# A streaming transformer kernel: the first stream unit's steps in another order on four engines

## Chip, cores, metric

One core of one Trainium2 chip. The metric is the device time of one execution of the whole program, in microseconds. It computes in fp32, with most products written as three matmuls of split operands (high by high, low by high, high by low).

## What is computed

Two layers of an encoder trunk. Each layer projects the hidden rows, attends in two head groups (latent attention over all cached keys, sliding-window attention with sinks), normalises and mixes the two results, adds the residual, and runs a SwiGLU feed-forward block. The part that the change touches is the attention of the eight running streams ("sample") and the output projection after it:

```
def _sample_layer(x, ckv_c, kr_c, k_c, v_c, p):
    q_lat, q_rope, ckv, kr, sq, sk, sv = _project(x, pos, w_in, q_g, w_uq, w_uk, kv_g)
    o_lat = _mla_attend(q_lat, q_rope, jnp.concatenate([ckv_c, ckv], axis=1),
                        jnp.concatenate([kr_c, kr], axis=1), None)
    o_swa = _swa_attend(sq, jnp.concatenate([k_c, sk], axis=1),
                        jnp.concatenate([v_c, sv], axis=1), sinks, None)
    y = _block_out(x, o_lat, o_swa, p)
...
def _block_out(x, o_lat, o_swa, p):
    o_a = jnp.einsum('bthl,lhv->bthv', o_lat, w_uv).reshape(b, t, MLA_OUT)
    mix = jnp.concatenate([rms_norm(o_a, g_a), rms_norm(o_swa, g_b)], axis=-1)
    x = layer_norm(ALPHA * x + jnp.einsum('btm,md->btd', mix, w_out), ln1_g, ln1_b)
...
```

## The kernel before

Each layer runs in stages: A projects ten row tiles, B attends for the eight prompt tiles, C (the stage of the change) attends for the streams, and then comes the feed-forward block. Stage C has nine units, n = 0 to 8. Unit 0 is the sixteen meta rows, which are short; units 1 to 8 are the eight streams, each with 1040 cached keys. Beside the attention of unit n, stage C multiplies row tile n-1 by `w_out` (1024 by 1024), so that TensorE (PE) has something to do during a softmax. The row tiles 0 to 7 are the prompt's, whose attention is done.

Every engine has its own program, written out by hand, and an engine executes in order: an instruction that waits holds up all that stands behind it. Nothing plans the order; it is the order of the calls at lines 2007 to 2047 (ScalarE, ACT), 2709 to 2752 (VectorE, DVE), 3471 to 3488 (PE) and 1328 to 1368 (SyncE, SP, which issues the loads). Engines wait for each other through counting semaphores. The steps, by the names of the helpers:

- `q_latent_hi/lo`, `q_turned` (ACT L1914, L1920, DVE L2566): the streams' queries are copied out of PSUM, as a high and a low part. `scores(0)` waits for all of them.
- `stream_keys`, `keys_hi`, `keys_lo`: keys of a unit are loaded (`dkraw`, `dsraw`), then split on ACT (`dkh`) and GpSimd (POOL, `dkl`). `four_rotary`, `rotary_hi`, `rotary_lo`, `stream_rotary`: the rotary keys of four units are loaded (`krraw`), split into `krh` on ACT and `krl` on DVE, and three DMAs of SP (L1269) copy the rows of one unit into `drs`. `scores(n)` for n of 1 and more waits for `drs` (semaphore `dr_in0` or `dr_in1`) and for `dkl`.
- `scores(n)` on PE (L3300); `bias(n)` on DVE (L2574, the row maxima; its last instruction writes `nbs`); `soft(n)` on ACT (L1926, the exponentials); `inverse(n)` on DVE (L2588, normalises `Pb`); `turn_probs(n)` on PE (L3342, transposes `Pb`); `turned_hi(n)` on ACT and `turned_lo(n)` on DVE (the split copy `PT`); `values(n)` on PE (L3351); `out_hi(n)` and `out_lo(n)`.
- `mix_load(s)`, `mix_sq(s)` (ACT), `mix_eps(s)` and `mix_norm(s)` (DVE, with a root on POOL between them), `mix_T(s)` on PE (L3393, eight transposes of `mt`), `mix_hi(s)` on ACT (`mTh`), `mix_lo(s)` on DVE (`mTl`): row tile s is normalised, turned and split for the output projection.
- `w_out_load(k)` on SP, `w_out_hi(n)` on ACT (L1954, writes `wouth`), `w_out_lo(n)` on DVE (L2699, writes `woutl`): the eight 128-row blocks of the matrix are loaded (`woraw`) and split. ACT waits for groups of blocks: the first three in the order of use have one semaphore. `w_out(s, k0, k1)` on PE (L3404) multiplies row tile s by blocks k0 to k1-1: six matmuls of 512 columns for a block. It waits for `mTl` and, in tile 0, for each block's `woutl`.
- `values_hi(b)` on ACT and `values_lo(b)` on POOL split the values of a stream (`dv`).

In units 1 to 8 PE executes `scores(n)`, `w_out(n-1, 0, 5)`, `turn_probs(n)`, `w_out(n-1, 5, 8)`, `values(n)`, `mix_T(n)`.

Of the kernel before, what the change touches and what calls it, by code (L numbers as in the profile page):

```python
# [96 lines left out]
def rows(t):  # L97
    return META if t == TILES - 1 else P
# [27 lines left out]
W_OUT_ORDER = (2, 3, 4, 5, 6, 0, 1, 7)  # L126
# [175 lines left out]
def program(nc, X, LNP, ROT, W_IN, QKVG, W_UQ, W_UK, W_UV, SINKS, MIXG, W_OUT, LN1, W_FF,  # L302
# [8 lines left out]
    with ExitStack() as ctx:  # L311
        names = {}

        def S(name):
            if name not in names:
                names[name] = ctx.enter_context(nc.semaphore(name))
            return names[name]
# [309 lines left out]
        def f(ap):  # L627
            return ap.bitcast(F32)
# [287 lines left out]
        def load_params(sp, l, which):  # L916
            for dst, src in small_loads(l, which):
                sp.dma_start(dst, src, allow_slow_non_contiguous=which == "C").then_inc(S("params_in"), 16)
# [4 lines left out]
        def params(eng, key):  # L923
            eng.wait_ge(S("params_in"), 16 * param_count[key])
# [213 lines left out]
        def _(sp):  # L1138
            for l in range(L):
# [71 lines left out]
                def mix_pair_store(x):  # L1211
                    p, s = PASSES[x][1] // 2, PASSES[x][1] % 2
                    sp.wait_ge(S("b_item_lo"), by_dve(l, ITEM["ot", x]))
                    dst = MIX[BANK * s:BANK * (s + 1), P * p:P * (p + 1)].rearrange("(t p) c -> p t c", p=P)
                    sp.dma_start(dst, mixP[:, :, :]).then_inc(S("b_mixP_out"), 16)
# [30 lines left out]
                def stream_keys(b):  # L1246
                    i = b % 2
                    sem = S(f"dm_in{i}")
                    if b >= 2:
                        sp.wait_ge(S("s_done"), U(l, b - 1) + 1)  # L1250
                    sp.dma_start(dkraw[i][:, :], CKVT[l, b]).then_inc(sem, 16)
                    for j in range(2):
                        sp.dma_start((dsraw[i] if b else dsraw0)[HD * j:HD * (j + 1), :, :],
                                     SKT[l, b].rearrange("(g d) n -> d g n", d=HD)).then_inc(sem, 16)
# [37 lines left out]
                def w_out_load(k):  # L1292
                    sp.dma_start(woraw[:, k, :], w_out_rows[:, k, :]).then_inc(S(f"wo_in{W_OUT_GROUP[k]}"), 16)

                def mix_load(s):
                    t, r = row_tile(s), rows(row_tile(s))
                    if 1 <= s < 9:
                        sp.wait_ge(S("c_ms"), A(l, s))
                        sp.wait_ge(S("c_mT"), A(l, s))
                    if s < 8:  # L1300
                        sp.dma_start(mt[:, :], MIX[cols(t), :]).then_inc(S("mt_in"), 16)
                        return

                    for i in range(2):
                        units = range(i, 1 if s == 8 else UNITS, 2)
                        sp.wait_ge(S(f"mixs_out{i}"), 16 * ([5, 4][i] * l + len(units)))
                    sp.dma_start((mt[0:r, 512:1024] if s == 8 else mtw[:, :]), MIX[cols(t), 512:1024])\
                      .then_inc(S("mt_in"), 16)
# [17 lines left out]
                            sp.wait_ge(S("s_done"), U(l, NB) + 1)  # L1326
                        sp.dma_start((xin, xin_late)[g][i][0:rows(t), :], H1[cols(t), :]).then_inc(S("xin_in"), 16)
                four_rotary(0)
                stream_keys(0)
                for i in range(2):  # L1330
                    sp.dma_start(f(sqT[i][:, :]), SQT[8 + i, :, 0:SWA_H * rows(8 + i)]).then_inc(S("sq_in"), 16)
                mix_load(0)
                load_params(sp, l, "E")
                for k in W_OUT_ORDER[0:2]:
                    w_out_load(k)
                sp.wait_ge(S("qa"), 2 * (l + 1))
                sp.wait_ge(S("qr"), 2 * (l + 1))
                sp.wait_ge(S("qa_rope"), 2 * (l + 1))
                sp.dma_start(mixg[:, :], MIXG[l:l + 1, :].to_broadcast([P, D])).then_inc(S("mixg_in"), 16)
                mix_pair_store(NPASS - 1)  # L1340
                stream_rotary(0)
                for k in W_OUT_ORDER[2:5]:
# [339 lines left out]
        def _(act):  # L1682
            for l in range(L):
# [200 lines left out]
                def keys_hi(b):  # L1884
                    i = b % 2
                    act.wait_ge(S(f"dm_in{i}"), 16 * 3 * (l * NB // 2 + b // 2 + 1))
                    act.activation(dkh[i][:, :], dkraw[i][:, :], ACT.Copy).then_inc(S("dm_hi"), 1)
                    act.activation(dsh[i][:, :, 0, :], (dsraw[i] if b else dsraw0)[:, :, :], ACT.Copy).then_inc(S("dw_hi"), 1)

                def rotary_hi(x):  # L1890
                    act.wait_ge(S("kr_in"), 16 * (2 * l + x + 1))
                    if x == 0:
                        act.wait_ge(S("qa"), 2 * (l + 1))
                        act.wait_ge(S("qr"), 2 * (l + 1))
                    act.activation(krh[:, :], krraw[:, :], ACT.Copy).then_inc(S("kr_hi"), 1)
# [46 lines left out]
                def turned_hi(n):  # L1942
                    if n >= 1:
                        act.wait_ge(S("pv"), U(l, n - 1) + 1)
                    for g in groups_of(n):
                        act.wait_ge(S("probsT"), G(l, n, g) + 1)
                        src, dst = turned(n, g, PT[:, 0, :])
                        act.activation(dst, src, ACT.Copy).then_inc(S("probsT_hi"), 1)
# [5 lines left out]
                def w_out_hi(n):  # L1954
                    k = W_OUT_ORDER[n]
                    act.wait_ge(S(f"wo_in{W_OUT_GROUP[k]}"), 16 * W_OUT_GROUP.count(W_OUT_GROUP[k]) * (l + 1))
                    act.activation(wouth[:, k, :], woraw[:, k, :], ACT.Copy).then_inc(S("wo_hi"), 1)

                def mix_sq(s):
                    r = rows(row_tile(s))  # L1960
                    act.wait_ge(S("mt_in"), 16 * (A(l, s) + 1))
                    parts = [mt[0:r, 0:512], mt[0:r, 512:1024]]
                    if s >= 8:
                        act.wait_ge(S("oa"), 2 * l + s - 7)
                        parts[0] = o_of(NB)[0:r, :]
                    if s == 9:
                        parts[1] = mtw[:, :]
                    junk = junkC[:, :].bitcast(mybir.dt.bfloat16)
                    for i in range(2):
                        ins = act.activation(junk[0:r, 512 * i:512 * i + 512], parts[i], ACT.Square,  # L1970
                                             scale=512 ** -0.5, accum_out=ms[s % 2][0:r, i:i + 1])
                    ins.then_inc(S("c_ms"), 1)

                def mix_hi(s):
                    r = rows(row_tile(s))
                    act.wait_ge(S("c_mT"), A(l, s) + 1)
                    if 1 <= s < 9:
                        act.wait_ge(S("c_y"), A(l, s))
                    act.activation(w_out_half(s)[0][:, :, 0:r], heads(OO, r), ACT.Copy).then_inc(S("c_mh"), 1)
# [32 lines left out]
                q_rope_hi(1)  # L2012
                act.wait_ge(S("phase_done"), 5 * phase_no(l, "B"))
                q_nope_hi(1)
                rotary_hi(0)
                q_latent_hi(0)
                keys_hi(0)
                q_turned(0)
                q_turned(1)
                q_latent_hi(1)  # L2020
                mix_sq(0)
                params(act, (l, "E"))
                soft(0)
                for k in range(2):
                    w_out_hi(k)
                turned_hi(0)
                mix_hi(0)
                out_hi(0)
                for k in range(2, 6):
                    w_out_hi(k)  # L2030
                for n in range(1, UNITS):
                    if n >= 2:
# [182 lines left out]
        def _(dve):  # L2215
# [13 lines left out]
            for l in range(L):  # L2229
# [484 lines left out]
                q_rope_lo(1)  # L2714
                dve.wait_ge(S("phase_done"), 5 * phase_no(l, "B"))
                q_nope_lo(1)
                rotary_lo(0)
                q_latent_lo(0)
                q_latent_lo(1)
                params(dve, (l, "E"))  # L2720
                dve.tensor_scalar(nsink[:, :], sinkT[:, 4:5], -1.0, None, ALU.mult).then_inc(S("nsinks"), 1)
                mix_eps(0)
                bias(0)
                mix_norm(0)
                inverse(0)
                w_out_lo(0)
                turned_lo(0)
                mix_lo(0)
                out_lo(0)
                for k in range(1, 5):  # L2730
                    w_out_lo(k)
                for n in range(1, UNITS):
                    if n >= 2:
# [232 lines left out]
        def _(pe):  # L2966
# [8 lines left out]
            for l in range(L):  # L2975
# [497 lines left out]
                q_latent(1)  # L3473
                for n in range(UNITS):
                    scores(n)
                    if n >= 1:
                        w_out(n - 1, 0, K_SOFT)
                    if n == NB:
                        project(1)
                    if n == 0:  # L3480
                        mix_T(0)
                    turn_probs(n)
                    if n >= 1:
                        w_out(n - 1, K_SOFT, KD)
                    values(n)
                    if n >= 1:
                        mix_T(n)
# [208 lines left out]
```

## Time and profile before

| | |
|---|---|
| median of 3 executions | 3064.08 us (3055.17 to 3064.78) |
| the profiled execution, its own time | 3059.69 us |
| its span | 3057.9 us |
| PE busy | 2896.3 us, 95% |
| DVE / ACT / POOL busy | 71% / 41% / 57% |
| TensorE's granted clock, mean | 0.973 |

Busy times are of one profiled execution; a busy PE is not PE at its peak. The granted clock is a share of 2.4 GHz: 1.00 is the full level and 0.50 the level of 1.2 GHz. Times in the rows below are in us from the start of the span. "Idle before" in brackets says how long the engine had stood and what ended that, with the releaser inferred from semaphores.

### The profile page before, as it was taken

The page shows a single profiled execution, that of the slowest core. Times are in us where ns is not written, and L with a number is a line of the kernel's source. Part 1 is how long each engine was busy: PE and PEld are TensorE (multiplying, and loading weights), DVE is VectorE, ACT ScalarE, POOL GpSimd, SP SyncE. Part 2 cuts the span into 40 slices and gives each one's busy share as a digit, 9 for nine tenths or more (in the row PEclk, how much of TensorE's full clock was granted, in tenths as well). Part 3 has the DMA queues.
Part 4 walks back from the last instruction along what each step waited for, and adds up shares of the span by engine and source line. Part 5 has one row for each costly group of instructions (what it writes and reads, how often), then busy time and mean ns, then how long its engine had stood idle before and what let it go on. Part 6 is the DMA issues. An engine that isn't in the chain of part 4 may idle for free.

```text
span 3057.9 us, 54602 instructions
## 1 busy us (share of the span) xinstructions
PE 2896.3 (95%) x20464; PEld 2639.4 (86%) x20464; DVE 2156.6 (71%) x3903; ACT 1256.0 (41%) x2474; POOL 1728.1 (57%) x1388
## 2 busy tenths in 40 slices
PE   7989997999999999999989899989999999999997
PEld 6966665887999999999989666668889999999997
DVE  6767777667777767778655677776577777678777
ACT  3334344445444434444333344444454444344442
POOL 2323333436777767888632233433277777678875
PEclk9989998999999999999989899989999999999998
DMA  4321114553333343333322211156432333433331
GB/s 168 135 86 51 44 40 158 162 161 111 108 105 106 109 164 134 107 104 109 127 93 97 87 42 42 36 173 180 148 116 96 109 110 107 182 111 114 101 104 57
DMA packets 193137, 336.06 MB, mean 110 GB/s; under 512 B 57200, under 2 KB 112752, under 8 KB 190800
## 3 DMA queue, kind: packets, MB, share of 16 engines
q1 hardware_dynamic: 166528, 276.94, 28.2%
q10 hardware_dynamic: 17248, 30.28, 2.7%
q0 software_dynamic: 9136, 25.89, 2.2%
q8 instruction: 135, 2.21, 0.3%
q14 instruction: 90, 0.74, 0.1%
HBM read 263.48 MB, written 65.52 MB: 108 GB/s over the span
## 4 chain that ended last, share of the span: by engine, by line
PE 79%; DVE 10%; issue 3%; ACT 2%; DMA 2%; POOL 2%; SPq 1%; POOLq 0%; DVEq 0%; ACTq 0%
PE PS L2969 23%; PE PS L2971 22%; PE PS L2970 22%; PE PS L3096 5%; DVE mxc L2466 2%; DVE Ph L2505 1%; POOL Pl L1555 1%; PE PS L3364 1%; DMA winraw<-in_W_IN 1%; DMA ht<-in_X 1%; PE PS L3257 1%; DMA woraw<-in_W_OUT 1%; PE PS L2989 0%; DVE T L2778 0%; PE PS L3347 0%
## 5 line engine op out<-in xcount | busy, mean ns | idle before, releaser
L1608 POOL TENSOR_TENSOR wopl<-T,woph 128x512 fp32r<-128x512 f32 x348 | 525.0, 1527 | 98.0 <-ACT woph L2066 97.0
L1555 POOL TENSOR_TENSOR Pl<-Pf,Ph 128x256 fp32r<-128x256 f32 (+5 forms) x174 | 218.9, 1265 | 366.4 <-DVE Ph L2505 366.4
L2969 PE MATMUL PS<-hidh,wdh 128*128 128x320 f32 (+1 forms) x1408 | 419.3, 298 | 5.4 <-DVE hidl L2783 4.4
L2971 PE MATMUL PS<-hidh,wdl 128*128 128x320 f32 (+1 forms) x1408 | 418.9, 298 | 0.0
L2970 PE MATMUL PS<-hidl,wdh 128*128 128x320 f32 (+1 forms) x1408 | 418.2, 297 | 0.0
L2066 ACT ACTIVATE woph<-T 128x512 fp32r<-128x512 f32 x348 | 216.6, 630 | 475.9 <-DVE T L2778 259.6
L2969 PE MATMUL PS<-xoh,woph 128*128 128x320 f32 x1232 | 383.1, 311 | 3.5 <-POOL wopl L1608 3.1
L2971 PE MATMUL PS<-xoh,wopl 128*128 128x320 f32 x1232 | 381.2, 309 | 0.0
L2970 PE MATMUL PS<-xol,woph 128*128 128x320 f32 x1232 | 380.5, 309 | 0.0
L2836 DVE TENSOR_TENSOR acc<-acc,PS 128x320 f32<-128x320 f32 (+1 forms) x608 | 275.4, 455 | 148.4 <-PE PS L2971 145.5
L2969 PE MATMUL PS<-x_both,woph 128*128 128x264 f32 x1232 | 349.9, 284 | 0.0
L2971 PE MATMUL PS<-x_both,wopl 128*128 128x264 f32 x1232 | 349.7, 284 | 0.0
L2970 PE MATMUL PS<-x_both,woph 128*128 128x264 f32 x1232 | 349.2, 283 | 0.0
L1615 POOL TENSOR_TENSOR wdl<-rd,wdh 128x512 fp32r<-128x512 f32 x176 | 256.7, 1478 | 30.3 <-ACT wdh L2075 30.3
L2969 PEld LDWEIGHTS PS<-hidh,wdh 128*128 128x128 f32 x1408 | 266.0, 189 | 7.7 <-issue 4.7
L2971 PEld LDWEIGHTS PS<-hidh,wdl 128*128 128x128 f32 x1408 | 265.9, 189 | 0.0
L2970 PEld LDWEIGHTS PS<-hidl,wdh 128*128 128x128 f32 x1408 | 265.8, 189 | 0.0
L1608 POOL TENSOR_TENSOR wopl<-rg,woph 128x512 fp32r<-128x512 f32 x128 | 178.9, 1399 | 130.3 <-ACT woph L2066 130.3
L1873 ACT ACTIVATE Pf<-PS 128x512 f32<-128x512 f32 (+5 forms) x174 | 127.8, 752 | 277.9 <-PE PS L3096 277.3
L2969 PEld LDWEIGHTS PS<-xoh,woph 128*128 128x128 f32 x1232 | 232.3, 189 | 6.0 <-POOL wopl L1608 4.9
L1608 POOL TENSOR_TENSOR wopl<-ru,woph 128x512 fp32r<-128x512 f32 x132 | 189.3, 1442 | 84.7 <-ACT woph L2066 82.3
L2970 PEld LDWEIGHTS PS<-xol,woph 128*128 128x128 f32 x1232 | 232.5, 189 | 0.2
(498 smaller groups left out, 7829.1 us busy)
## 6 DMA issues: line engine op xcount, KB each, us to landing
ru<-in_W_FF SPq DMA_DIRECT2D x88, 512.0 KB, 4.3
rd<-in_W_FF SPq DMA_DIRECT2D x176, 256.0 KB, 2.7
rg<-in_W_FF SPq DMA_DIRECT2D x82, 512.0 KB, 4.2
xs_scratch<-x_part ACTq DMA_DIRECT2D x56, 264.0 KB, 2.5
x_both<-xs_scratch ACTq DMA_DIRECT2D x14, 1056.0 KB, 7.8
sqt_scratch<-sqTs POOLq DMA_DIRECT2D x18, 512.0 KB, 4.6
hc<-out_H SPq DMA_DIRECT2D x18, 512.0 KB, 3.7
dkraw<-in_CKVT SPq DMA_DIRECT2D x16, 520.0 KB, 4.5
```

What stands on the lines that cost most here:

```text
L1555: ins = pool.tensor_tensor(Pl[i][0:kk, 1, c], Pf[i][0:kk, 1, c], f(Ph[i][0:kk, 1, c]), ALU.subtract)
L1608: pool.tensor_tensor(wopl[k][:, :, :], w_whole(w, k, first), f(woph[k][:, :, :]), ALU.subtract)\
L1615: pool.tensor_tensor(wdl[:, n, e, :], rd[n][:, :, :], f(wdh[:, n, e, :]), ALU.subtract)\
L1873: ins = act.activation(Pf[r][0:kk, :, c], both_banks(u)[0:kk, :, c], ACT.Exp)
L2066: act.activation(woph[k][:, :, :], w_whole(w, k, first or second), ACT.Copy).then_inc(S("f_hi"), 1)
L2466: dve.tensor_reduce(mxc[s][:, u["tl"], :, u["c"]], both_banks(u)[:, :, 0:u["c1"] - u["c0"]], AX.X, ALU.max, negate=True).then_inc(S("b_ite ...
L2505: ins = dve.tensor_copy(Ph[r][0:kk, :, c], Pf[r][0:kk, :, c])
L2836: dve.tensor_tensor(a, a, down_bank(u, g), ALU.add).then_inc(S("f_y"), 1)
L2969: pe.matmul(out, wh, mh, start=start, stop=False)
L2970: pe.matmul(out, wh, ml, start=False, stop=False)
L2971: return pe.matmul(out, wl, mh, start=False, stop=stop)
L3096: ins = pe.matmul(out(h), w(rows_, h), x(rows_, h), start=start and n == 0, stop=stop and n == len(passes) - 1)
```

## The change

It reorders calls, in both layers, and adds or removes none. On SP, the streams' window queries `sqT` are loaded ahead of the first keys, the sink parameters ahead of `mt`, and `mixg` ahead of the first two blocks of `w_out`. On ACT, the rotary and key splits go behind the query copies, `mix_sq(0)` behind `soft(0)`, and the first two `w_out_hi` to the other six, behind `mix_hi(0)`; `out_hi(0)` now stands ahead of `mix_hi(0)`. On DVE, `rotary_lo(0)` goes behind the query copies, `bias(0)` and `inverse(0)` ahead of the mix tile's steps, `out_lo(0)` ahead of `mix_lo(0)`, and the first `w_out_lo` to the other four, behind `mix_lo(0)`. On PE, `mix_T(0)` moves from behind `scores(0)` to behind `scores(1)`.

```
@@ SP
                 four_rotary(0)
-                stream_keys(0)
                 for i in range(2):
                     sp.dma_start(f(sqT[i][:, :]), SQT[8 + i, :, 0:SWA_H * rows(8 + i)]).then_inc(S("sq_in"), 16)
+                stream_keys(0)
+                load_params(sp, l, "E")
                 mix_load(0)
-                load_params(sp, l, "E")
-                for k in W_OUT_ORDER[0:2]:
-                    w_out_load(k)
                 ...
                 sp.dma_start(mixg[:, :], MIXG[l:l + 1, :].to_broadcast([P, D])).then_inc(S("mixg_in"), 16)
+                for k in W_OUT_ORDER[0:2]:
+                    w_out_load(k)
                 mix_pair_store(NPASS - 1)
                 stream_rotary(0)
@@ ACT
-                rotary_hi(0)
                 q_latent_hi(0)
-                keys_hi(0)
                 q_turned(0)
                 q_turned(1)
                 q_latent_hi(1)
-                mix_sq(0)
+                rotary_hi(0)
+                keys_hi(0)
                 params(act, (l, "E"))
                 soft(0)
-                for k in range(2):
-                    w_out_hi(k)
+                mix_sq(0)
                 turned_hi(0)
+                out_hi(0)
                 mix_hi(0)
-                out_hi(0)
-                for k in range(2, 6):
+                for k in range(6):
                     w_out_hi(k)
@@ DVE
-                rotary_lo(0)
                 q_latent_lo(0)
                 q_latent_lo(1)
+                rotary_lo(0)
                 params(dve, (l, "E"))
                 ...
+                bias(0)
+                inverse(0)
                 mix_eps(0)
-                bias(0)
+                turned_lo(0)
                 mix_norm(0)
-                inverse(0)
-                w_out_lo(0)
-                turned_lo(0)
+                out_lo(0)
                 mix_lo(0)
-                out_lo(0)
-                for k in range(1, 5):
+                for k in range(5):
                     w_out_lo(k)
                 for n in range(1, UNITS):
@@ PE
                 for n in range(UNITS):
                     scores(n)
+                    if n == 1:
+                        mix_T(0)
                     if n >= 1:
                         w_out(n - 1, 0, K_SOFT)
                     if n == NB:
                         project(1)
-                    if n == 0:
-                        mix_T(0)
                     turn_probs(n)
```

The rows of three places follow, in the program of layer 0; buffer numbers stand behind names. PE first, from the last matmuls of `scores(0)` to those of `scores(1)`. Before:

```order
L3320 MATMUL PS<-krT,qrT_175 128x16
L3401 MATMUL PS<-ident,mt 128x128 [waits qb_lo,c_mixn]
L3401 MATMUL PS<-ident,mt 128x128 x7
L3347 MATMUL PS<-ident,Pb 16x128 [waits pnorm]
L3347 MATMUL PS<-ident,Pb 16x128
L3364 MATMUL PS<-PT,v_74 128x256 [waits probsT_lo]
```

Now, from the end of `scores(1)`:

```order
L3317 MATMUL PS<-drs_208,qrT_174 128x512
L3398 MATMUL PS<-ident,mt 128x128 [waits qb_lo,c_mixn]
L3398 MATMUL PS<-ident,mt 128x128 x7
L2966 MATMUL PS<-wouth,mTh 128x512 [waits wo_rest,qc_out,c_ml]
L2967 MATMUL PS<-woutl,mTh 128x512
```

The transposes of `mt` stand behind the last matmul of `scores(1)` and directly ahead of `w_out(0, 0, 5)`, which needs what ACT and DVE make of them.

ACT from `soft(0)` to `soft(1)` (the two rows with `Pb,sums`). Before:

```order
L1934 ACTIVATE Pb,sums_195<-PS,mx_191 128x16 [waits bias,params_in]
L1935 ACTIVATE eed_197<-sinkT,nbs_193 128x1
L1938 ACTIVATE Pb,sums_195<-PS,nbs_193 64x16 x2
L1957 ACTIVATE wouth<-woraw 128x1024 [waits wo_in0] x2
L1948 ACTIVATE PT<-PS 16x2x128 [waits probsT]
L1979 ACTIVATE mTh<-PS 128x1024 [waits c_mT]
L1952 ACTIVATE ol_182<-PS 128x128 [waits pv]
L1957 ACTIVATE wouth<-woraw 128x1024 [waits wo_in0]
L1957 ACTIVATE wouth<-woraw 128x1024 [waits wo_in1] x3
L1957 ACTIVATE wouth<-woraw 128x1024 [waits wo_in2] x2
L1934 ACTIVATE Pb,sums_196<-PS,mx_192 128x1056 [waits probsT,bias]
```

Now:

```order
L1934 ACTIVATE Pb,sums_195<-PS,mx_191 128x16 [waits bias,params_in]
L1935 ACTIVATE eed_197<-sinkT,nbs_193 128x1
L1938 ACTIVATE Pb,sums_195<-PS,nbs_193 64x16 x2
L1970 ACTIVATE junkC,ms_62<-mt 128x512 [waits mt_in]
L1970 ACTIVATE junkC,ms_62<-mt 128x512
L1948 ACTIVATE PT<-PS 16x2x128 [waits probsT]
L1952 ACTIVATE ol_182<-PS 128x128 [waits pv]
L1979 ACTIVATE mTh<-PS 128x1024 [waits c_mT]
L1957 ACTIVATE wouth<-woraw 128x1024 [waits wo_in0] x3
L1957 ACTIVATE wouth<-woraw 128x1024 [waits wo_in1] x3
L1957 ACTIVATE wouth<-woraw 128x1024 [waits wo_in2] x2
L1934 ACTIVATE Pb,sums_196<-PS,mx_192 128x1056 [waits probsT,bias]
```

All eight `wouth` copies now stand behind the copy `mTh`, which waits for `mix_T(0)` (`c_mT`).

DVE from `mTl` to the end of `bias(1)`. Before:

```order
L2644 TENSOR_TENSOR mTl<-PS,mTh 128x1024 [waits c_mh]
L2612 TENSOR_SCALAR mixs_189<-PS,rin_199 64x64 [waits ol_hi]
L2612 TENSOR_SCALAR mixs_189<-PS,rin_199 64x64
L2616 TENSOR_TENSOR orest<-PS,ol_182 128x128
L2618 TENSOR_TENSOR ol_183<-PS,orest 128x128 [waits o_rest]
L2702 TENSOR_TENSOR woutl<-woraw,wouth 128x1024 [waits wo_hi] x4
L2581 TENSOR_REDUCE mx_192<-PS 64x1 [waits s_done]
L2581 TENSOR_REDUCE mx_192<-PS 64x1
L2583 TENSOR_REDUCE mx_192<-PS 128x1
L2586 TENSOR_TENSOR nbs_194<-mx_192,nsink 128x1 [waits mx,nsinks]
```

Now:

```order
L2642 TENSOR_TENSOR mTl<-PS,mTh 128x1024 [waits c_mh]
L2700 TENSOR_TENSOR woutl<-woraw,wouth 128x1024 [waits wo_hi] x5
L2579 TENSOR_REDUCE mx_192<-PS 64x1 [waits s_done]
L2579 TENSOR_REDUCE mx_192<-PS 64x1
L2581 TENSOR_REDUCE mx_192<-PS 128x1
L2584 TENSOR_TENSOR nbs_194<-mx_192,nsink 128x1 [waits mx,nsinks]
```

Between `mTl` and `bias(1)` there are five blocks of `woutl` instead of four, and `mTl` itself now waits for a copy that comes after `scores(1)`.

## Rows read from the trace of the kernel before

**Rows 1.** The page, busy time and count by engine

```profile
PE 2896.3 (95%) x20464; PEld 2639.4 (86%) x20464; DVE 2156.6 (71%) x3903; ACT 1256.0 (41%) x2474; POOL 1728.1 (57%) x1388
```

**Rows 2.** Timeline of PE, layer 0: start, duration, instruction, idle before

```profile
514.10 1.97 PE L3401 MATMUL PS<-ident,mt 128*128 128x128 f32 x8 [3.10 <-DVE mt L2636]
...
520.65 0.70 PE L3327 MATMUL PS<-dsh,sqT 128*128 128x144 f32 x2
...
527.45 0.39 PE L2969 MATMUL PS<-wouth,mTh 128*128 128x512 f32 x1
...
534.45 1.36 PE L3347 MATMUL PS<-ident,Pb 128*128 128x128 f32 x11
```

**Rows 3.** Timeline of ACT, layer 0

```profile
511.76 0.27 ACT L1934 ACTIVATE Pb<-PS,mx 128x16 f32<-128x16 f32 x1 [1.97 <-DVE nbs L2586]
...
516.50 2.00 ACT L1957 ACTIVATE wouth<-woraw 128x1024 fp32r<-128x1024 f32 x2 [3.56 <-DMA woraw<-in_W_OUT]
...
518.80 1.00 ACT L1979 ACTIVATE mTh<-PS 128x1024 fp32r<-128x1024 f32 x1
...
520.93 5.78 ACT L1957 ACTIVATE wouth<-woraw 128x1024 fp32r<-128x1024 f32 x6
529.70 1.15 ACT L1934 ACTIVATE Pb<-PS,mx 128x1056 f32<-128x1056 f32 x1 [2.99 <-DVE nbs L2586]
```

**Rows 4.** Timeline of DVE, layer 0

```profile
519.83 1.23 DVE L2644 TENSOR_TENSOR mTl<-PS,mTh 128x1024 fp32r<-128x1024 f32 x1 [0.49 <-ACT mTh L1979]
...
522.19 4.62 DVE L2702 TENSOR_TENSOR woutl<-woraw,wouth 128x1024 fp32r<-128x1024 f32 x4
527.65 0.66 DVE L2581 TENSOR_REDUCE mx<-PS 64x1 f32<-64x160 f32 x2 [0.84 <-PE PS L3320]
...
532.41 0.77 DVE L2596 TENSOR_SCALAR Pb<-Pb,rin 128x1056 f32<-128x1056 f32 x1
```

**Rows 5.** The chain of waits in layer 0 behind `soft(1)`: start, duration, what

```profile
533.47 3.92 POOL dv L1571
```

**Rows 6.** Windows, layer 0: span, its us, busy us by engine, granted clock, DMA share, GB/s

```profile
504.00:509.00 5.00, 0.01 (x2) 0.00 (x0) 2.85 (x8) 4.43 (x13) 2.76 (x2) 0.77 1.01 364
...
519.40:527.20 7.80, 7.80 (x28) 7.02 (x29) 6.91 (x9) 6.36 (x8) 0.00 (x0) 0.50 1.10 338
527.20:534.00 6.80, 6.80 (x31) 5.47 (x30) 5.02 (x9) 4.26 (x9) 0.53 (x1) 1.00 1.06 285
...
566.00:670.00 104.00, 104.00 (x598) 89.29 (x598) 64.44 (x123) 45.69 (x96) 43.86 (x31) 1.00 0.53 160
```

**Rows 7.** SP's issues in layer 0; the landings of sinkT and drs

```profile
503.46 0.43 SPq L918 DMA_DIRECT2D sinkT<-in_SINKS  x1
DMA to landing us min/median/max: 5.1/5.1/5.1
...
507.31 0.59 SPq L1269 DMA_DIRECT2D drs<-krl  x1
DMA to landing us min/median/max: 8.0/8.0/8.0
```

**Rows 8.** The same in layer 1: drs, scores(1), end of bias(1)

```profile
2020.55 0.59 SPq L1269 DMA_DIRECT2D drs<-krl  x1
DMA to landing us min/median/max: 6.9/7.4/7.8
...
2033.61 0.70 PE L3327 MATMUL PS<-dsh,sqT 128*128 128x144 f32 x2
...
2042.71 0.15 DVE L2586 TENSOR_TENSOR nbs<-mx,nsink 128x1 f32<-128x1 f32 x1
```

**Rows 9.** Timeline of PE, layer 0, unit 2's scores at the full clock

```profile
543.70 1.09 PE L3401 MATMUL PS<-ident,mt 128*128 128x128 f32 x8
544.55 0.42 PE L3327 MATMUL PS<-dsh,sqT 128*128 128x144 f32 x2
...
549.21 0.50 PE L2969 MATMUL PS<-wouth,mTh 128*128 128x512 f32 x1 [0.77 <-DVE mTl L2644]
```

## The prediction

> **What bounds the kernel now.** I read the page first: PE is busy for 2896.3 of 3057.9 us [rows 1], so time can be won or lost only where PE stands or where its work is pushed back. Then the windows around stage C: from 566 to 670 PE is busy for 104.00 of 104.00 us [rows 6]. Units 2 to 8 leave no gap, and whatever shifts their start shifts the end of the kernel by the same amount. So the change is worth what it does to the start of unit 2, once in each layer.
>
> The timelines show how unit 1 is reached. PE starts `scores(1)` at 520.65 and is at `w_out(0, 0, 5)` by 527.45 [rows 2]. Ahead of it PE idled, because ACT stood 3.56 us for the blocks of `w_out` and copied two of them in 2.00 us before it split the turned probabilities of unit 0 [rows 3]. Over 504 to 509 PE did nothing and its granted clock fell; `scores(1)` ran at 0.50, and `w_out(0)` at 1.00 again [rows 6]. `bias(1)` follows `scores(1)` at once, at 527.65 [rows 4]; its end releases `soft(1)` at 529.70, for which ACT had stood 2.99 us, with all eight `wouth` copies done [rows 3]. Behind `soft(1)` the chain of waits runs over POOL, which splits the values from 533.47 to 537.39 [rows 5] and then makes the next keys' low part and the root for the next mix tile, and over DVE to `mTl`, for which PE waits 0.77 us at 549.21 [rows 9]. **The end of bias(1) therefore times the start of unit 2.**
>
> **What the front part gains.** SP's reordering, the query copies ahead of the rotary and key splits, and unit 0's softmax ahead of the mix tile bring `values(0)` forward. `bias(0)` needs the sink parameters. They landed at 503.46 + 5.1 = 508.6 [rows 7] and are issued one short slot earlier, so I take 508.1, with 0.8 us for `bias(0)`: `soft(0)` starts at 508.9 instead of 511.76 [rows 3]. From there to the end of `values(0)`, where `scores(1)` starts at 520.65 [rows 2], it was 8.9 us. Without the 5.56 us of waiting and copying for `w_out`, and with about 1.3 us for the two squares of `mix_sq(0)` that now stand there (two passes over 512 columns, an estimate from half a 1.00 us copy of 1024 columns each [rows 3] and the read of the sum), it is 4.7. So `values(0)` ends at 513.6, some 7 us earlier.
>
> But `scores(1)` also needs the rotary rows `drs`. Their last DMA was issued at 507.31 and landed 8.0 us later, at 515.3 [rows 7]: not because of itself, but because 16 DMA engines were busy all the time [rows 6] and it stood behind megabytes of other loads. The change alters the order among these loads; the same bytes still stand ahead of `drs`. It is issued about a microsecond later, since `krl` is made later, which the backlog hides. I take **515.3** for the start of `scores(1)`, 5.3 us earlier than before. In layer 1 the landing is 2020.55 + 7.8 = 2028.4 against a start at 2033.61 [rows 8]: 5.2 us earlier.
>
> **What the back part costs.** Before, `mTh`, `mTl`, all `wouth` and the first five `woutl` lay under the wait for `w_out` and under `scores(1)`; that cover is gone, since the eight transposes of `mt` now stand behind `scores(1)`. ACT stands at `mTh` with eight `wouth` copies and `soft(1)` behind it. DVE stands at `mTl` with five `woutl` and `bias(1)` behind it. In layer 0, from the landing of `drs`:
>
> - `scores(1)`, at the half clock as before, 520.65 to 527.45 [rows 2]: 6.8, to 522.1
> - `mix_T(0)`, at the half clock 1.97 [rows 2]: to 524.1
> - `mTh` 1.00 [rows 3], `mTl` 1.23 [rows 4]: to 526.3
> - five `woutl` at 4.62 / 4 = 1.155 [rows 4]: 5.8, to 532.1. ACT's eight `wouth` at 5.78 / 6 = 0.96 [rows 3] run ahead of them and end at 525.1 + 7.7 = 532.8, before `soft(1)` is wanted
> - `bias(1)`, from 527.65 [rows 4] to the start of `soft(1)` at 529.70 [rows 3]: 2.05, and 0.1 for the hand-overs: to 534.2
>
> That is 534.2 against 529.7: **4.5 us later**, although `scores(1)` is 5.3 earlier. The 18.9 us counted from `drs` put layer 1 at 2028.4 + 18.9 = 2047.3 against 2042.71 + 0.15 = 2042.9 [rows 8]: 4.4 later. Everything behind has its old distance: the last two `woutl` beside POOL's split of `dv`, the turned probabilities, `values(1)`.
>
> PE is not the bound in between. Its five blocks of `w_out(0)` took 534.45 - 527.45 = 7.0 us [rows 2]; they start with the first `woutl`, at 527.5, and `turn_probs(1)` cannot start before about 537.7 (4.5 behind 532.41 + 0.77 = 533.2, when `Pb` was ready [rows 4]). They have 10.2 us, enough even if the first part runs at the half clock. SP's next `mt` load waits for `mix_T(0)`, done at 524.1, before SP comes to it; this costs nothing. If its cover were gone, it would be by these 2 us at most.
>
> Sum: 4.5 + 4.4 = 8.9, with nothing to set against it, since units 2 to 8 have no slack. On the profiled execution that is 3059.69 + 8.9 = 3068.6; the median of the runs shown stands 4.4 above that execution, so by it 3073.0. I take the middle of the two, rounded down, **3070**.
>
> **Unknown costs, from both sides.** The clock under `scores(1)` and `mix_T(0)`: at 1.00 they take 3.9 (544.55 to 548.44) and about 1.0 us [rows 9], 3.8 less. I take the half clock, since PE has only `scores(0)`, two transposes and `values(0)` to do between 504 and 515, all of them short, and the row nearest to that, 504 to 509, shows the fall [rows 6]. The landing of `drs`: from `values(0)`'s 513.6 to about 516.6, if the later issue does shift it.
>
> **Rivals.**
>
> A, on the other side: **the clock stays full.** PE's long gap is cut into short ones, the fall never comes, and `scores(1)` with `mix_T(0)` are 3.8 us shorter. Then the layers lose 0.7 and 0.6 us: 3061.0 by the profiled execution, not slower by any measurement. For it: the gaps are 1 to 3 us. Against it: PE is mostly idle all the same. It decides if the granted clock over `scores(1)` is 1.00. Chance 0.15.
>
> B: **drs is not late.** A rotary DMA is small, and with the keys asked for in another order it may land before `values(0)` ends. `scores(1)` starts at 513.6, 1.7 us per layer better: 8.9 - 3.4 = 5.5, so 3065.2. Against it: the 8.0 us above. The Trainium skill says, in "DMA: Bandwidth & Descriptors", section "Anatomy of one DMA", that a DMA costs about 2.0 us of fixed time and its bytes at 436 GB/s; by that rule `drs`, issued by about 509, would be there by about 511 and this rival would hold. The trace disagrees while a backlog stands in the queue: 8.0 us for 32 rows of 1040 fp32, 133 KB. Chance 0.12. With A and B both, the sum is 1.3 - 3.4 = -2.1: 3057.6.
>
> C: **PE becomes the bound at the half clock.** After `mix_T(0)` PE waits some 3.4 us for the first `woutl`. If the clock is then low through all of `w_out(0)`, the five blocks take 14.0 instead of 7.0 and end at 541.5, and the transposes and the last three blocks take 2.4 + 8.4 more, to 552.3. At the full clock they took 1.36 and, at 1.4 a block, 4.2 from 534.45 [rows 2], to 540.0, which the forecast moves to 544.5. That is 7.8 more in each layer: 3059.7 + 8.9 + 15.6 = 3084. Against it: in the rows the clock rose during `scores(1)`, within the 7.8 us of unbroken work from 519.4 to 527.2 [rows 6]. Chance 0.10.
>
> D: **something outside this account**, in either direction, such as a DMA that lands differently in stage C or a shift that later work takes up. Against it speaks the unbroken 104 us. Chance 0.13, spread from -10 to +15 us.
>
> The forecast itself has 0.50.
>
> **Numbers.** A measurement of this kernel can tell about 0.3%, 9.2 us, from no change, and the forecast of 8.9 stands right at that bound: I split its 0.50 into 0.24 slower, 0.24 same, 0.02 faster. A gives 0.13 same, 0.02 faster; B 0.10 same, 0.02 slower; C 0.10 slower; D 0.07 same, 0.04 faster, 0.02 slower. Together 0.08 faster, 0.54 same, 0.38 slower. The range runs from 3058 (A with B) to 3082 (most of C, or the forecast with the scatter of the runs); it leaves out less than 2 in 10.
>
> **What would show it.** Right: in both layers `scores(1)` starts at 515 to 516 (2028 to 2029) directly on the landing of `drs`; ACT idles before `mTh` until about 524 with the releaser PE L3398; DVE idles before `mTl`; `bias(1)` ends some 12 us behind `scores(1)` instead of 2; `w_out(0)` stops block by block for `woutl`; unit 2's `mTl` is 4 to 5 us later than before. Wrong: `bias(1)` ends before 530, the clock over `scores(1)` is 1.00, or unit 2 starts at its old place although `bias(1)` is late.

## The result and the profile after

| | before | changed |
|---|---|---|
| median of the runs | 3063.99 us (20 runs, 3053.55 to 3075.63) | 3075.68 us (20 runs, 3064.94 to 3082.31) |
| ratio, with its 95% interval | | 1.0033 [1.0024, 1.0043] |
| the profiled execution, its own time | 3059.69 us | 3080.32 us |
| its span | 3057.9 us | 3078.5 us |
| granted clock of TensorE, mean | 0.973 | 0.970 |

The kernel became slower by a third of a per cent: about 10 us by the ratio, 11.7 us between the two medians. The forecast was 8.9 us. The page says little of why:

```profile
PE 2910.2 (95%) x20464; PEld 2647.0 (86%) x20464; DVE 2158.7 (70%) x3903; ACT 1255.5 (41%) x2474; POOL 1726.9 (56%) x1388
```

The counts are those of [rows 1]. PE's busy time has grown by 13.9 us with no matmul added, so part of the difference between these two executions is clock and none of it work.

**A common zero.** The two profiled executions are 20.6 us apart, nearly twice what the medians are, so times from the start of the span can't be compared. The first load of stage C, SP's `krraw` in each layer, is untouched by the change and is my zero. It was issued at 499.70 and 2011.99 before, and at 509.20 and 2026.73 after. 9.5 of the 20.6 us had therefore passed before the changed code began. In that stretch the windows view shows the same work at another mean clock: 0.96 before, in its first row, and 0.94 after:

```profile
0.00:499.70 499.70, 443.68 (x3126) 354.78 (x3127) 350.74 (x685) 185.18 (x402) 175.72 (x211) 0.96 0.25 81
```

```profile
0.00:509.20 509.20, 453.36 (x3123) 361.76 (x3124) 350.10 (x685) 184.72 (x400) 174.96 (x211) 0.94 0.25 80
```

PE's busy time is 9.7 us longer there, and that of the other engines is not. This is scatter between executions; what the change does is read from the zero on.

**PE in layer 0 of the changed kernel**, timeline:

```profile
523.73 0.57 PE L3361 MATMUL PS<-PT,v 16*128 16x256 f32 x1 [0.91 <-DVE PT L2601]
...
525.56 0.68 PE L3324 MATMUL PS<-dsh,sqT 128*128 128x144 f32 x2 [0.51 <-issue]
...
532.53 1.91 PE L3398 MATMUL PS<-ident,mt 128*128 128x128 f32 x8
...
538.03 0.47 PE L2966 MATMUL PS<-wouth,mTh 128*128 128x512 f32 x1 [3.60 <-DVE woutl L2700]
...
547.92 1.42 PE L3344 MATMUL PS<-ident,Pb 128*128 128x128 f32 x11 [1.12 <-DVE Pb L2594]
...
563.91 0.50 PE L2966 MATMUL PS<-wouth,mTh 128*128 128x512 f32 x1 [0.76 <-DVE mTl L2642]
```

`values(0)` starts 14.5 us behind the zero instead of 19.7, and `scores(1)` at 525.56 - 509.20 = 16.4 instead of 20.95 [rows 2]: the front part works. Then the transposes of `mt` stand behind `scores(1)`, PE idles 3.60 us for the first `woutl`, and `turn_probs(1)` waits 1.12 us for `Pb`, which shows that PE was done with its five blocks of `w_out(0)` and is not the bound. The last row is the place of [rows 9] where unit 2 waits for `mTl`: 54.7 us behind the zero instead of 49.5, which is **5.2 us later**.

**What ACT and DVE do in between**, the same layer, ACT first:

```profile
534.47 1.02 ACT L1979 ACTIVATE mTh<-PS 128x1024 fp32r<-128x1024 f32 x1 [9.11 <-PE PS L3398]
535.39 7.67 ACT L1957 ACTIVATE wouth<-woraw 128x1024 fp32r<-128x1024 f32 x8
544.38 1.15 ACT L1934 ACTIVATE Pb<-PS,mx 128x1056 f32<-128x1056 f32 x1 [1.32 <-DVE nbs L2584]
```

```profile
535.53 1.23 DVE L2642 TENSOR_TENSOR mTl<-PS,mTh 128x1024 fp32r<-128x1024 f32 x1 [8.92 <-ACT mTh L1979]
536.67 5.76 DVE L2700 TENSOR_TENSOR woutl<-woraw,wouth 128x1024 fp32r<-128x1024 f32 x5
542.34 0.65 DVE L2579 TENSOR_REDUCE mx<-PS 64x1 f32<-64x160 f32 x2
...
544.20 0.15 DVE L2584 TENSOR_TENSOR nbs<-mx,nsink 128x1 f32<-128x1 f32 x1
```

ACT stands 9.11 us in front of `mTh` and DVE 8.92 us in front of `mTl`, both for the eight transposes. `scores(1)` had ended by 532.53, but `bias(1)` starts at 542.34, behind `mTl` and the five `woutl`; before, it started with the end of `scores(1)` [rows 4]. `soft(1)` still waits for `nbs`, as in [rows 3].

**Layer 1**, PE, then ACT:

```profile
2043.45 0.67 PE L3324 MATMUL PS<-dsh,sqT 128*128 128x144 f32 x2 [0.29 <-issue]
...
2050.42 1.09 PE L3398 MATMUL PS<-ident,mt 128*128 128x128 f32 x8
...
2080.95 0.50 PE L2966 MATMUL PS<-wouth,mTh 128*128 128x512 f32 x1 [0.76 <-DVE mTl L2642]
```

```profile
2051.55 1.02 ACT L1979 ACTIVATE mTh<-PS 128x1024 fp32r<-128x1024 f32 x1 [8.07 <-PE PS L3398]
...
2061.46 1.14 ACT L1934 ACTIVATE Pb<-PS,mx 128x1056 f32<-128x1056 f32 x1 [1.32 <-DVE nbs L2584]
```

`soft(1)` starts 34.73 us behind the zero, against 30.90 before: 3.8 us later. The last PE row, unit 2's wait for `mTl`, is as much later. Nothing takes the two shifts up: from that wait in layer 0 to the first transpose of `xin`, behind stage C (688.1 before, 702.8 after), PE needs 138.9 us in both kernels, and from there it is 1323.9 us to the zero of layer 1 in both. From the wait in layer 1 to the end, the changed execution takes 2.0 us more (997.55 against 995.51), 1.7 of them behind stage C, where nothing was changed; what they are was not traced.

So at `soft(1)` the layers lose 5.18 + 3.83 = **9.0 us**. With the 9.5 ahead of the first zero and these 2.0 at the end, that makes up the 20.6 us between the two executions.

### The profile page after: what moved, and what is told of

It is laid out like the page before. It is cut to its first block, busy times and chain, and to the rows that moved or that the text cites. A ratio compares the mean times of both kernels' runs of the same rounds, so it can differ in the third digit from the quotient of the medians.

```text
span 3078.5 us, 54602 instructions
## 1 busy us (share of the span) xinstructions
PE 2910.2 (95%) x20464; PEld 2647.0 (86%) x20464; DVE 2158.7 (70%) x3903; ACT 1255.5 (41%) x2474; POOL 1726.9 (56%) x1388
## 4 chain that ended last, share of the span: by engine, by line
PE 81%; DVE 9%; issue 3%; ACT 2%; POOL 2%; DMA 2%; POOLq 0%; SPq 0%; DVEq 0%; ACTq 0%
PE PS L2966 23%; PE PS L2968 22%; PE PS L2967 22%; PE PS L3093 5%; DVE mxc L2464 1%; POOL Pl L1555 1%; PE PS L3361 1%; DVE Ph L2503 1%; DMA winraw<-in_W_IN 1%; PE PS L3254 1%; DMA ht<-in_X 1%; PE PS L2986 1%; PE PS L3398 1%; PE PS L3344 1%; ACT Pf L1873 0%
```

## The experiments

Each ran several times beside the kernel before. Beside the ratio I read the start of `soft(1)` behind the zero, in both layers, since unit 2 follows it: `scores(2)` starts 14.8 to 15.1 us behind it in every trace but that of experiment 3 (15.8 and 15.9) and layer 0 of experiment 6 (16.1), where `w_out(0)` keeps PE busy longer. It was 30.00 and 30.90 before, 35.18 and 34.73 in the changed kernel. Each such time comes from one profiled execution, and where the front part is the same code, `scores(1)` still starts up to 0.5 us earlier or 0.7 us later than in the changed kernel (experiments 3 and 6).

**1. PE's part of the change alone.** The kernel before, with `mix_T(0)` moved:

```
@@ PE, in the kernel before
                     scores(n)
+                    if n == 1:
+                        mix_T(0)
...
-                    if n == 0:
-                        mix_T(0)
                     turn_probs(n)
```

> The kernel before with the PE part of the change alone: mix_T(0) behind scores(1). Theory (the cover is gone): scores(1) starts where it did, 21.0 us behind the first load of stage C in layer 0, and then mix_T 1.97, mTh 1.00, mTl 1.23, the rest of out_lo(0) 1.2 and four woutl 4.6 stand between scores(1) and bias(1), about 10 us per layer: 20 us slower than before, ratio 1.0065. Rival (the reordered loads and copies on SP, ACT and DVE are what costs): no change, ratio 1.000 within 0.001.

Measured: 3085.5 us, ratio 1.0070 [1.0054, 1.0085]; `soft(1)` at 39.81 and 40.17, so 9.8 and 9.3 us later than before. ACT in layer 0, and DVE's `mTl`:

```profile
520.47 2.00 ACT L1957 ACTIVATE wouth<-woraw 128x1024 fp32r<-128x1024 f32 x2 [3.36 <-DMA woraw<-in_W_OUT]
...
533.57 1.02 ACT L1979 ACTIVATE mTh<-PS 128x1024 fp32r<-128x1024 f32 x1 [10.70 <-PE PS L3401]
534.64 5.79 ACT L1957 ACTIVATE wouth<-woraw 128x1024 fp32r<-128x1024 f32 x6
543.46 1.14 ACT L1934 ACTIVATE Pb<-PS,mx 128x1056 f32<-128x1056 f32 x1 [3.03 <-DVE nbs L2586]
```

```profile
534.62 1.22 DVE L2644 TENSOR_TENSOR mTl<-PS,mTh 128x1024 fp32r<-128x1024 f32 x1 [11.31 <-ACT mTh L1979]
```

The move on PE costs twice what the whole change costs. The other engines' parts give half of it back.

**2. The change without its back part.** PE turns the mix tile behind `values(0)`, as it does in every other unit:

```
@@ PE, in the changed kernel
                     scores(n)
-                    if n == 1:
-                        mix_T(0)
...
                     values(n)
-                    if n >= 1:
-                        mix_T(n)
+                    mix_T(n)
```

> The changed kernel with mix_T(0) turned behind values(0), ahead of scores(1), and all else of the change kept. Theory: mt is ready about when values(0) ends, mix_T costs scores(1) some 1.5 us of start, but mTh, mTl and woutl are again covered by it. soft(1) then starts about 28.2 us behind the first load (before 30.0, changed 35.2), 1.8 us earlier than before in each layer: 3.6 us faster than before, ratio 0.9988, and 12 us faster than the changed kernel. Rival (the reordered loads and copies cost): as slow as the changed kernel, ratio 1.003.

Measured: 3057.19 us, ratio 0.9980 [0.9971, 0.9989]; `soft(1)` at 27.58 and 28.26, 2.4 and 2.6 us earlier than before. **This kernel is faster than both**: its interval lies below 1 and below that of the changed kernel. PE, then DVE, in layer 0:

```profile
515.43 1.97 PE L3398 MATMUL PS<-ident,mt 128*128 128x128 f32 x8
517.05 0.68 PE L3324 MATMUL PS<-dsh,sqT 128*128 128x144 f32 x2
```

```profile
518.49 1.23 DVE L2642 TENSOR_TENSOR mTl<-PS,mTh 128x1024 fp32r<-128x1024 f32 x1 [1.50 <-ACT mTh L1979]
519.63 5.75 DVE L2700 TENSOR_TENSOR woutl<-woraw,wouth 128x1024 fp32r<-128x1024 f32 x5
525.30 0.65 DVE L2579 TENSOR_REDUCE mx<-PS 64x1 f32<-64x160 f32 x2
```

The same five copies take the same 5.75 us, but from 519.63 on, while PE computes `scores(1)` from 517.05. `bias(1)` comes 8.3 us behind the start of `scores(1)`, in the changed kernel 16.8.

**3. bias(1) ahead of the five blocks.** Everything else as changed:

```
@@ DVE, in the changed kernel
                 mix_lo(0)
+                bias(1)
                 for k in range(5):
                     w_out_lo(k)
                 for n in range(1, UNITS):
                     if n >= 2:
                         mix_lo(n - 1)
-                    bias(n)
+                        bias(n)
```

> The changed kernel with bias(1) ahead of the five woutl on DVE. If DVE's five blocks alone held up the softmax, soft(1) would start 5.8 us per layer earlier than in the changed kernel, ratio to before 0.9995. By the theory ACT's queue is the next bound: eight wouth end 1.3 us before soft(1) starts in the changed kernel, so only 1.3 us per layer come back, ratio to before 1.0025.

Measured: 3069.01 us, ratio 1.0019 [1.0008, 1.0029]; `soft(1)` at 33.29 and 34.29. DVE and ACT, layer 0:

```profile
529.63 0.65 DVE L2579 TENSOR_REDUCE mx<-PS 64x1 f32<-64x160 f32 x2
...
531.48 0.15 DVE L2584 TENSOR_TENSOR nbs<-mx,nsink 128x1 f32<-128x1 f32 x1
```

```profile
527.43 1.02 ACT L1979 ACTIVATE mTh<-PS 128x1024 fp32r<-128x1024 f32 x1 [9.42 <-PE PS L3399]
528.35 7.67 ACT L1957 ACTIVATE wouth<-woraw 128x1024 fp32r<-128x1024 f32 x8
535.92 1.12 ACT L1934 ACTIVATE Pb<-PS,mx 128x1056 f32<-128x1056 f32 x1
```

`nbs` is there at 531.6, but ACT starts `soft(1)` at 535.92, without an idle moment before it: its eight `wouth` copies are next in line. The loss stands in two queues, and taking it out of DVE's alone gives 1.9 and 0.4 us. Counted from the start of `scores(1)`, `soft(1)` comes 17.4 us later in both layers, against 18.8 and 18.0 in the changed kernel; in layer 1 `mix_T(0)` ran at the half clock here (1.91 us) and not there (1.09 us). With that taken out it is 1.4 us in either layer, close to the 1.3 expected.

**4. The blocks of w_out moved, nothing else.** The kernel before, with the ACT and DVE blocks where the change has them:

```
@@ ACT, in the kernel before
                 soft(0)
-                for k in range(2):
-                    w_out_hi(k)
                 turned_hi(0)
                 mix_hi(0)
                 out_hi(0)
-                for k in range(2, 6):
+                for k in range(6):
                     w_out_hi(k)
@@ DVE
                 inverse(0)
-                w_out_lo(0)
                 turned_lo(0)
                 mix_lo(0)
                 out_lo(0)
-                for k in range(1, 5):
+                for k in range(5):
                     w_out_lo(k)
```

> The kernel before with one part of the change: on ACT and DVE the first blocks of w_out go behind the mix tile's copies; mix_T(0) and all loads stay. Theory: the 3.56 + 2.00 us at wouth leave unit 0's chain, so turned_hi(0) goes on the end of its own transposes, 1.9 us earlier, scores(1) too, and bias(1) 1.5 to 1.9 us earlier per layer: 3 to 4 us faster, ratio 0.9989. Rival (w_out's blocks are needed early): w_out(0) then waits for woutl and nothing is gained, ratio 1.000 or above.

Measured: 3061.59 us, ratio 0.9994 [0.9982, 1.0006]; `soft(1)` at 28.44 and 30.11, so 1.6 and 0.8 us earlier. The time alone settles nothing, since its interval holds 1; the trace has the direction that was expected. It is less than half of what experiment 2 gains; the rest comes from the other parts of the change, SP's reordering and the earlier `soft(0)` among them, which were not tried one by one.

**5. Four blocks ahead of bias(1) instead of five**, on top of experiment 2:

```
@@ DVE, in the kernel of experiment 2
                 mix_lo(0)
-                for k in range(5):
+                for k in range(4):
                     w_out_lo(k)
...
                     if n == 1:
+                        w_out_lo(4)
                         w_out_lo(5)
```

> The kernel of e2 (mix_T(0) behind values(0)) with four woutl blocks instead of five ahead of bias(1) on DVE; the fifth goes behind it. In e2 DVE came to bias(1) 1.2 us after scores(1) had ended. Theory (DVE's queue ahead of bias(1) times unit 2): bias(1) follows scores(1) at once, soft(1) 0.8 to 1.2 us earlier than in e2, bounded then by ACT's eight wouth, which end 26.8 us behind the first load: about 2 us faster than e2, ratio to before 0.9974. Rival (PE is the bound in e2): as e2, 0.998.

Measured: 3058.49 us, ratio 0.9981 [0.9969, 0.9993]; `soft(1)` at 27.57 and 27.54. Against experiment 2 that is 0.0 and 0.7 us, less than I expected. DVE in layer 0:

```profile
522.92 4.64 DVE L2700 TENSOR_TENSOR woutl<-woraw,wouth 128x1024 fp32r<-128x1024 f32 x4
527.54 0.66 DVE L2579 TENSOR_REDUCE mx<-PS 64x1 f32<-64x160 f32 x2
```

One block fewer takes 1.1 us off DVE, but in this execution `mt` and with it `scores(1)` came 0.6 us later behind the zero (17.91 against 17.28). DVE's four blocks and `scores(1)` now end together, so `bias(1)` has no more to win from a shorter queue. ACT's queue comes next, as expected: in layer 0 `nbs` is there at 529.41 + 0.15 = 529.56, and `soft(1)` starts at 529.99 without an idle moment behind the `wouth` copies:

```profile
529.99 1.12 ACT L1934 ACTIVATE Pb<-PS,mx 128x1056 f32<-128x1056 f32 x1
```

**6. The blocks ahead of mTh and mTl**, PE's order as changed:

```
@@ ACT, in the changed kernel
                 out_hi(0)
-                mix_hi(0)
                 for k in range(6):
                     w_out_hi(k)
+                mix_hi(0)
@@ DVE
-                mix_lo(0)
                 for k in range(5):
                     w_out_lo(k)
+                mix_lo(0)
```

> The changed kernel, PE's order kept (mix_T(0) behind scores(1)), with the first six wouth and five woutl ahead of mTh and mTl instead of behind. Theory: of the 5.3 us that soft(1) lost, the five blocks (5.8 us) come back, the transposes, mTh and mTl (4.2 us) stay between scores(1) and bias(1): soft(1) starts 29.6 us behind the first load, as before the change (30.0), ratio to before 0.9997 (up to 1.0006 if w_out(0) begins at the half clock). Rival (the late transposes alone are the cost, whatever ACT and DVE do): ratio stays near 1.003.

Measured: 3063.42 us, ratio 0.9997 [0.9985, 1.0008]; `soft(1)` at 29.27 and 30.60. DVE, then PE, layer 0:

```profile
530.45 1.22 DVE L2642 TENSOR_TENSOR mTl<-PS,mTh 128x1024 fp32r<-128x1024 f32 x1 [0.44 <-ACT mTh L1979]
531.60 0.65 DVE L2579 TENSOR_REDUCE mx<-PS 64x1 f32<-64x160 f32 x2
```

```profile
531.73 0.80 PE L2966 MATMUL PS<-wouth,mTh 128*128 128x512 f32 x1 [2.52 <-DVE mTl L2642]
```

PE turns the mix tile as late as in the changed kernel, and the loss is gone. It was the copies behind the wait: with the five `woutl` on DVE and six of the eight `wouth` on ACT ahead of it, 5.9 and 4.1 us come back. Counted from the start of `scores(1)` it is 6.4 and 4.8 us, and with the clock under `mix_T(0)` taken out (1.04 and 1.91 us here, 1.91 and 1.09 in the changed kernel) 5.5 and 5.6, close to the 5.8 of the five copies. What is left behind `scores(1)`, the transposes with `mTh` and `mTl`, is paid for by the earlier start of `scores(1)`. That start came 0.5 and 0.7 us later than in the changed kernel, from identical code: PE's clock was already low under the query transposes (2.69 us for the sixteen of `qrs` in both layers, against 1.55), `soft(0)` came 2.3 us later and `values(0)` 1.1.

**7. What holds drs.** The first two blocks of `w_out` are loaded behind the rotary rows instead of ahead of them:

```
@@ SP, in the changed kernel
                 sp.dma_start(mixg[:, :], MIXG[l:l + 1, :].to_broadcast([P, D])).then_inc(S("mixg_in"), 16)
-                for k in W_OUT_ORDER[0:2]:
-                    w_out_load(k)
                 mix_pair_store(NPASS - 1)
                 stream_rotary(0)
-                for k in W_OUT_ORDER[2:5]:
+                for k in W_OUT_ORDER[0:5]:
                     w_out_load(k)
```

> The changed kernel, with the first two blocks of w_out loaded behind the rotary rows drs of unit 1 instead of ahead of them; the order on PE, ACT and DVE is the changed kernel's. Theory (drs is late in the changed kernel because of the megabytes that stand ahead of it): 1.05 MB fewer stand ahead, 2.9 us at the 358 GB/s of the window over scores(1), so the last drs lands 4.2 to 5 us behind its issue instead of 7.2 and 8.0; scores(1) then starts at once behind values(0), 0.4 to 1 us earlier (15.4 to 16.0 us behind the first rotary load), and soft(1) moves by the same 0.4 to 1 us, since nothing else on its way changes; the time of the kernel by 1 to 2 us, too little to tell: ratio to before 1.0028. The blocks of w_out arrive some 3 us later and are not missed, since no copy wants them before mTh. Rival (the 7 to 8 us are the DMA's own time, or the time of a small-row transfer): the landing stays at 7 to 8 us, scores(1) at 16.4 and 16.7 behind the first rotary load, and soft(1) does not move.

Measured: 3073.68 us, ratio 1.0026 [1.0013, 1.0039]; `soft(1)` at 34.22 and 33.95. SP's issue of the last `drs` DMA in layer 0, and under it the landings of the last two of unit 1 (us from issue to landing: least, median, most), in the changed kernel:

```profile
518.27 0.59 SPq L1269 DMA_DIRECT2D drs<-krl  x1
...
DMA to landing us min/median/max: 6.7/6.9/7.2
```

and in this one:

```profile
509.38 0.60 SPq L1269 DMA_DIRECT2D drs<-krl  x1
...
DMA to landing us min/median/max: 4.0/4.1/4.1
```

The same DMA lands in 4.1 us instead of 7.2 (layer 1: 4.8 instead of 8.0). `scores(1)` starts 15.49 and 16.13 us behind the zero instead of 16.36 and 16.72, now right behind `values(0)`, and `soft(1)` comes 1.0 and 0.8 us earlier. The two blocks ahead of `drs` made 3.1 and 3.2 us of its landing, and without them it is no longer what `scores(1)` waits for. The 4.1 and 4.8 us that are left, with other loads still ahead, were not parted further.

**All of them together.** The shift of `soft(1)`, summed over both layers, gives a ratio when it is divided by 3064 us. Nothing else is put in:

| kernel | soft(1), both layers, us | ratio from that | measured |
|---|---|---|---|
| 1, PE's part alone | +19.1 | 1.0062 | 1.0070 [1.0054, 1.0085] |
| the changed kernel | +9.0 | 1.0029 | 1.0033 [1.0024, 1.0043] |
| 7, rotary rows first | +7.3 | 1.0024 | 1.0026 [1.0013, 1.0039] |
| 3, bias(1) first | +6.7 | 1.0022 | 1.0019 [1.0008, 1.0029] |
| 6, blocks first | -1.0 | 0.9997 | 0.9997 [0.9985, 1.0008] |
| 4, blocks moved only | -2.4 | 0.9992 | 0.9994 [0.9982, 1.0006] |
| 2, mix tile ahead | -5.1 | 0.9983 | 0.9980 [0.9971, 0.9989] |
| 5, four blocks | -5.8 | 0.9981 | 0.9981 [0.9969, 0.9993] |

Eight kernels, and each measured interval holds the ratio that one instruction's start gives. Read at the first transpose of `xin` instead, behind stage C, the shifts are 2.1 us larger for experiment 1 (21.1, a ratio of 1.0069) and at most 1.1 us larger for the others, and all intervals hold those ratios too. So the account is closed at the 0.1% that these runs can tell, and no finer.

## Why the prediction was right

**What bounds the kernel: right.** `soft(1)` times unit 2, and no unit behind it takes a shift up, as the table shows. It is not always the end of `bias(1)` that releases it, as the forecast had it: in experiment 3 and in layer 0 of experiment 5 it was ACT's queue.

**The front part: right in size, partly by luck, two terms off.** I had `scores(1)` at 515.3 - 499.70 = 15.6 us behind the zero and 16.4 in layer 1; it came at 16.4 and 16.7. The landing of `drs` was 7.2 and 8.0 us, against the 8.0 and 7.8 taken; it was issued 1.5 us later behind the zero than before in layer 0, and I had let the backlog hide that. `values(0)` was further off. I had it end at 13.9, and experiment 7, where nothing else holds `scores(1)`, shows 15.5. The first term that failed is "`soft(0)` starts at 508.9", 9.2 behind the zero: it started at 519.11 - 509.20 = 9.9. The sink parameters, issued 0.6 us earlier behind the zero, landed 5.7 us later and not 5.1, so that `nbs` was ready at 9.5; and `keys_hi(0)` now stood ahead of `soft(0)` on ACT and waited for a load that had itself moved behind `sqT`:

```profile
517.80 1.07 ACT L1887 ACTIVATE dkh<-dkraw 128x1040 fp32r<-128x1040 f32 x1 [2.11 <-DMA dsraw_first<-in_SKT]
```

After it, DVE's `sums` took 1.11 us where it took 0.15 before. That `values(0)` was late cost next to nothing, which was luck: `scores(1)` goes by the later of the two, and `drs` was later still.

**The back part: right.** I had `soft(1)` 18.9 us behind the landing of `drs`. Counted from the start of `scores(1)` it was 18.8 in layer 0 and 18.0 in layer 1. The steps in layer 0, forecast and measured: `scores(1)` 6.8 and 7.0, `mix_T(0)` with `mTh` and `mTl` 4.2 and 4.1, five `woutl` 5.8 and 5.7, `bias(1)` with its hand-overs 2.15 and 2.0. In layer 1 the clock had risen by the time of `mix_T(0)`, which took 1.09 us instead of the 1.97 I had, and that is why this layer lost 3.8 and not 4.4. Layer 0 lost 5.2 and not 4.5, by the later start. The two errors have opposite signs, and that they cancel, 9.0 against 8.9, is luck.

**The rivals.** A (the clock stays full) fell: over `scores(1)` the windows of the changed kernel show a clock of 0.50, in the first row here. C was half there: in the second row PE's clock is low once more under `w_out(0)`, after the idle 3.60 us.

```profile
525.50:532.50 7.00, 6.94 (x24) 6.12 (x25) 1.05 (x4) 0.00 (x0) 0.00 (x0) 0.50 1.03 398
538.20:542.20 4.00, 4.00 (x11) 3.11 (x11) 4.00 (x4) 4.00 (x6) 0.00 (x0) 0.57 1.03 319
```

It was down for some 3.5 us and cost nothing, since `turn_probs(1)` waited for `Pb` all the same. B fell as well, by the 7.2 us. The rule of the Trainium skill by which it would have held ("DMA: Bandwidth & Descriptors", section "Anatomy of one DMA") has a DMA take a fixed 2.0 us and its bytes at 436 GB/s. That section gives it for a DMA that GpSimd issues, and `drs` is issued by SP, which the prediction passed over. By an estimate from that rule the 133 KB of `drs` take 2.3 us; the shortest of all landings of `drs` in stage C was 3.0 us, before and after. In experiment 7 it is 4.1 us with 1.05 MB fewer ahead and 7.2 with them, so at least 3.1 of the 7.2 us are the backlog's. B's price was too high, too: `drs` was worth 1.0 and 0.8 us and not 1.7 a layer, because `values(0)` was later than I had it.

**The absolute time** of 3070 is 5.7 us below the median of 3075.7. The sum is not to blame. I based it on the middle between one profiled execution and three runs, while 20 runs put the kernel before at 3064.0; from there the sum gives 3072.9. The rest is within the interval of the ratio. The chances of the outcomes were added up wrongly: the terms as written give 0.10 faster, 0.54 same and 0.36 slower, and not 0.08 and 0.38; neither the sum nor the range hangs on that.

**What I had not seen** is that the two halves of the change can be parted. I wrote that the cover was gone, and priced that, but took the gain at the front for spent. Experiment 2 shows that it is there to be had: 5 us below the kernel before, 14 us at `soft(1)` below the changed one.

## What to carry to other kernels

On an engine that executes in order, a wait costs what is queued behind it, so before a step is moved later, list on each engine that uses its output what stands between that wait and the next thing on the critical path: here eight transposes of 2 us, moved by one place on PE, put 5.8 us of copies in front of `bias(1)`. Work that fills a gap is best put ahead of a late wait and not behind it, and the step that releases it belongs where the engines already wait for something else. Compare two executions from a common event that the change can't touch; here the span alone would have said 20.6 us for a change worth 9.

## What was not expected of the hardware

- **The clock's scatter outweighs the change.** The same instructions took 499.7 us in one execution and 509.2 in another, with PE's mean granted clock at 0.96 and 0.94 and the other engines' busy times equal. In experiment 6 the granted clock was 0.50 under the query products and transposes of both layers, in the changed kernel 1.00, with the same code there. What sets it was not tried.
- **DVE beside POOL.** A `woutl` copy takes 5.76 / 5 = 1.15 us while POOL is idle. The last two, which run while POOL splits `dv`, take 5.39 us together in the changed kernel, 2.7 each; the tiny `sums` takes 1.11 us instead of 0.15 beside POOL's `dkl`. DVE, then POOL, in the changed kernel:

```profile
520.30 1.11 DVE L2589 TENSOR_TENSOR sums<-sums,eed 128x1 f32<-128x1 f32 x1 [1.60 <-ACT Pb L1938]
...
547.78 5.39 DVE L2700 TENSOR_TENSOR woutl<-woraw,wouth 128x1024 fp32r<-128x1024 f32 x2
```

```profile
519.02 2.38 POOL L1563 TENSOR_TENSOR dkl<-dkraw,dkh 128x1040 fp32r<-128x1040 f32 x1 [15.09 <-ACT dkh L1887]
```

  That the two engines hold each other up is what these rows suggest; no run here parted them.
- **A small DMA lands later by what stands ahead of it.** 1.05 MB ahead of `drs` made 3.1 us of its 7.2 in layer 0 and 3.2 of its 8.0 in layer 1, which is 330 to 340 GB/s, about the rate at which this stretch moved bytes before the change (338 GB/s, [rows 6]).
